# Second-table row sums over the whole TensorE array: two products a row instead of four quarters and a fold

## The reference, cut to what matters

```
def peer_ffn(h, w_q, sub_keys, u_tab, v_tab):
    blocks = h.reshape(-1, PEER_BLOCK, d)          # blocks of 128 rows
    def one_block(xb):
        q = (xb @ w_q).reshape(PEER_BLOCK, PEER_HEADS, 2, PEER_HALF)
        ...
        act = jax.nn.gelu(jnp.einsum('thkd,td->thk', u_tab[idx], xb)) * wts
        return jnp.einsum('thk,thkd->td', act, v_tab[idx])
    return lax.map(one_block, blocks).reshape(bsz, t, d)
```

## Time and profile before

| | |
|---|---|
| median of three runs | 3575.82 us |
| span of the profiled execution | 3751.8 us |
| mean granted TensorE clock in it | 0.819 |
| busy: TensorE, VectorE, ScalarE, GpSimd | 2608.3, 1998.1, 710.4, 1507.8 us |
| HBM read | 1152.84 MB, of which the software queue (gathers above all) 849.51 MB |

### The profile page before, as it was taken

How to read it: one execution, slowest core, us unless ns; L and a number is a source line. 1 busy time by engine, 2 the same in 40 slices (tenths; PEclk the granted TensorE clock), 3 DMA queues, 4 the chain that set the end, 5 groups by cost and what they waited for, 6 DMA issues and landing times.

```text
span 3751.8 us, 35602 instructions
## 1 busy us (share of the span) xinstructions
PE 2608.3 (70%) x12888; PEld 1195.8 (32%) x12888; DVE 1998.1 (53%) x5016; ACT 710.4 (19%) x1775; POOL 1507.8 (40%) x1609
## 2 busy tenths in 40 slices
PE   6687766655556675655679666556654798899998
PEld 1233222111112221111144221112311385676765
DVE  0465656656657656776422476667698436221411
ACT  1121111211112311211132112112221213020300
POOL 0025555555665666566600056666466400000000
PEclk8888888788776887676679778777877899999999
DMA  8779998999998999899923489999999776667677
GB/s 316 269 275 342 342 344 326 367 402 401 365 361 320 356 363 340 320 364 361 359 100 122 149 326 384 361 364 332 348 354 334 298 260 255 219 251 249 215 255 258
DMA packets 363676, 1156.38 MB, mean 308 GB/s; under 512 B 33712, under 2 KB 33968, under 8 KB 362476
## 3 DMA queue, kind: packets, MB, share of 16 engines
q0 software_dynamic: 232144, 849.51, 60.5%
q1 hardware_dynamic: 130940, 304.36, 22.7%
q10 hardware_dynamic: 416, 0.23, 0.0%
HBM read 1152.84 MB, written 1.15 MB: 308 GB/s over the span
## 4 chain that ended last, share of the span: by engine, by line
PE 42%; DVE 19%; DMA 14%; issue 7%; POOL 7%; another core or an unknown queue 5%; ACT 5%; SPq 0%; DVEq 0%; ACTq 0%; POOLq 0%
PE PS L1155 10%; PE PS L1089 8%; POOL BIG L2357 7%; DVE BIG L1965 7%; PE PS L1360 6%; PE PS L1378 6%; DMA BIG<-in_p_v_dram,IDX 6%; DMA BIG<-in_p_u_dram,IDX 5%; PE PS L1254 2%; PE PS L1348 1%; PE PS L1117 1%; DVE SC L2151 1%; DMA WR<-in_w_mod_dram 1%; ACT dg L1552 1%
## 5 line engine op out<-in xcount | busy, mean ns | idle before, releaser
L1155 PE MATMUL PS<-BIG,dg 64*64 64x512 f32 x6144 | 1059.3, 823 | 849.7 <-ACT dg L1552 383.5
L2357 POOL DMA_INDIRECT BIG<-in_p_u_dram,IDX x768 | 734.5, 956 | 1163.2 <-ACT PS L1539 417.8
L1965 DVE CUSTOM_DVE_ANT_0 BIG<-BIG,PS 128x1024 f32<-128x1024 f32 x768 | 927.8, 1215 | 325.8 <-DMA BIG<-in_p_u_dram,IDX 294.3
L2357 POOL DMA_INDIRECT BIG<-in_p_v_dram,IDX x768 | 732.0, 953 | 313.7 <-issue 180.6
L1155 PEld LDWEIGHTS PS<-BIG,dg 64*64 64x64 f32 x6144 | 274.9, 172 | 1520.9 <-issue 963.4
L1089 PE MATMUL PS<-WR,HT 128*128 128x512 f32 x640 | 294.4, 614 | 9.9 <-DMA WR<-in_a_w_in_dram 6.6
L1552 ACT ACTIVATE dg<-twin,ACTV 128x64 f32<-128x64 f32 x768 | 208.0, 336 | 345.2 <-PE PS L1155 149.8
L1360 PE MATMUL PS<-HT,WR 128*128 128x128 f32 x2048 | 256.1, 285 | 5.9 <-DMA WR<-in_mlp_w_dram 5.9
L1360 PEld LDWEIGHTS PS<-HT,WR 128*128 128x128 f32 x2048 | 247.3, 200 | 15.8 <-issue 8.9
L1378 PE MATMUL PS<-WR,BIG 128*128 128x512 f32 x512 | 226.0, 596 | 0.0
L1089 PEld LDWEIGHTS PS<-WR,HT 128*128 128x128 f32 x640 | 122.3, 196 | 177.0 <-issue 167.9
(11 more groups left out here) (320 smaller groups left out, 2709.7 us busy)
## 6 DMA issues: line engine op xcount, KB each, us to landing
WR<-in_mlp_w_dram SPq DMA_DIRECT2D x128, 1024.0 KB
WR<-in_w_mod_dram SPq DMA_DIRECT2D x48, 1024.0 KB
WR<-in_b_w_in_dram SPq DMA_DIRECT2D x18, 1024.0 KB
WR<-in_a_w_in_dram SPq DMA_DIRECT2D x16, 1024.0 KB
WR<-in_p_w_q_dram SPq DMA_DIRECT2D x16, 1024.0 KB
BIG<-in_dsa_w_dram POOLq DMA_DIRECT2D x16, 1024.0 KB, 7.6
BIG<-in_p_u_dram,IDX POOLq DMA_INDIRECT x768
BIG<-in_p_v_dram,IDX POOLq DMA_INDIRECT x768
```

The source lines that it names most:

```text
L1155: mm = self.e.matmul(pv[64 * i:64 * i + 64, 2 * r + n, :], dg[p, :], row[p, n * 512:n * 512 + 512], start=h == 0 and j == 0, stop=h == 7 a ...
L1965: self.e.tensor_tensor_reduce(row, row, xp, 1.0, 0.0, ALU.mult, ALU.add, m.ACTV[:, u % 4, j:j + 1]).then_inc(*self.done("dot", l, u, j))
L2357: self.e.indirect_dma_start(row, None, m.A[f"p_{table}"], bass.IndirectOffsetOnAxis(ap=m.IDX[:, u % 4, j:j + 1], axis=0)).then_inc(*m.GR.l ...
```

## The change

A v-row is summed alone, over the whole array: `dg` is the full 128x128 diagonal (from `ident`), and there are two products of 128x128 by 128x512 a row, one for each half of the width. They add into one PSUM buffer of two banks a block; there are two such buffers, so `PV` has two places. `twin` is gone, and `dg` has five buffers of 512 bytes a partition instead of six of 256. The fold is gone on ScalarE and VectorE; `gated_add` reads the sum from PSUM itself, one step later than the fold stood. The scratch of the software DMA queue shrinks to 8192 bytes a partition, where no size was given before.

```
-        self.PV = Slots([PSt[:, 4:8, :]])
+        self.PV = Slots([PSt[:, 4 + 2 * i:6 + 2 * i, :] for i in range(2)])
...
-        self.DG = Slots([sb(f"dg{i}", [128, 64]) for i in range(6)])
+        self.DG = Slots([sb(f"dg{i}", [128, 128]) for i in range(5)])
...
     def finish(self, l, b, gate, gain, shift):
         m = self.m
-        for n in range(2):
-            self.fold(l, b, n)
         self.spread(gate, "b")
...
                     self.v_gather(l, u - 1, j)
-                    if j % 2:
-                        self.v_sum(l, u - 1, j - 1, b, h)
+                    self.v_sum(l, u - 1, j, b, h)
...
-        pv = m.PV.of(l, b)
-        self.wait_ge(m.act.at("diagonal", l, u, j + 1), m.GR.landed("v", l, u, j), m.GR.landed("v", l, u, j + 1))
+        pv, row, dg = m.PV.of(l, b), m.GR.of("v", l, u, j), m.DG.of(l, u, j)
+        self.wait_ge(m.act.at("diagonal", l, u, j), m.GR.landed("v", l, u, j))
         for n in range(2):
-            for i in range(2):
-                row, dg = m.GR.of("v", l, u, j + i), m.DG.of(l, u, j + i)
-                for r in range(2):
-                    p = slice(64 * r, 64 * r + 64)
-                    mm = self.e.matmul(pv[64 * i:64 * i + 64, 2 * r + n, :], dg[p, :],
-                                       row[p, n * 512:n * 512 + 512], start=h == 0 and j == 0,
-                                       stop=h == 7 and j == 14)
+            mm = self.e.matmul(pv[:, n, :], dg[:, :], row[:, n * 512:n * 512 + 512], start=h == 0 and j == 0,
+                               stop=h == 7 and j == 15)
...
+        m.GR.free(("v", l, u, j), self.done.last())
+        m.DG.free((l, u, j), self.done.last())
...
+            self.e.tensor_tensor(t, m.PV.of(l, b)[:, n, :], m.BC.of(*gate)[:, n0:n0 + 512], ALU.mult).then_inc(
+                *self.done())
...
-    nc = _bacc.Bacc("TRN2", target_bir_lowering=False, num_devices=1)
+    nc = _bacc.Bacc("TRN2", target_bir_lowering=False, num_devices=1, dynamic_dma_scratch_size=8192)
```

More of the change, by code:

```diff
@@ L143, in __init__ @@
         self.ones = sb("ones", [128, 128])
-        self.twin = sb("twin", [128, 64])
         self.iota16 = sb("iota16", [128, 16])
@@ L327 @@
     route_pick = route_which = route_hot = route_index = route_weights = block_begin = hold = nothing
-    activate = u_gather = v_gather = u_dot = v_sum = fold = tiles = gate_rows = gate_sums = nothing
+    activate = u_gather = v_gather = u_dot = v_sum = tiles = gate_rows = gate_sums = nothing
     ctx_decay = ctx_flip = ctx_state = lat_begin = lat_decay = lat_flip = lat_scaled = lat_scores = nothing
@@ L962, in mlp_first @@
         yield
-        self.wait_ge(self.m.dve.at("folded", 1, 1, 1))
+        self.wait_ge(self.m.dve.at("added", "sum", 1, 1, 1))
         for _ in zip(range(12), mlp):
@@ L1548, in v_sum @@
         m = self.m
[L1549 to L1558, removed]
-        self.wait_ge(m.pe.at("block sum", l, b), m.dve.at("tmp free", l, b))
-        self.e.activation(m.tmp[0:64, n, :], pv[64:128, n, :], ACT.Copy).then_inc(*self.done())
-        self.e.activation(m.tmp[64:128, n, :], pv[0:64, 2 + n, :], ACT.Copy).then_inc(*self.done("fold", l, b, n))
+        dg = m.DG.take(l, u, j)
+        self.wait_ge(m.dve.at("active", l, u), *m.DG.emptied(l, u, j))
+        self.e.activation(dg[:, :], m.ident[:, :], ACT.Copy, scale=m.ACTV[:, u % 4, j:j + 1]).then_inc(
+            *self.done("diagonal", l, u, j))
     def gate_rows(self, b, j, gs):
@@ L1774, in silu @@
         m = self.m
-        self.e.tensor_tensor(m.twin[:, :], m.ident[:, 0:64], m.ident[:, 64:128], ALU.add).then_inc(*self.done("twin"))
         self.wait_ge(m.act.at("silu"))
@@ L1851, in spatial_gate @@
         m.PS.free(("spatial", use, b, hh), self.done.last())
-    def fold(self, l, b, n):
-        m = self.m
-        pv = m.PV.of(l, b)
-        if not n:
-            self.done.note("tmp free", l, b)
-        for r in range(2):
-            p = slice(64 * r, 64 * r + 64)
-            t = m.tmp[p, n, :]
-            self.wait_ge(m.act.at("fold", l, b, n), m.pe.at("block sum", l, b))
-            self.e.tensor_tensor(t, t, pv[p, 2 * r + n, :], ALU.add).then_inc(*self.done("folded", l, b, n))
-        if n:
-            m.PV.free((l, b), self.done.last())
     def gated_add(self, name, b, n0, gate, last):
@@ L1870, in gated_add @@
         if name[0] == "sum":
-            self.e.tensor_tensor(t, t, m.BC.of(*gate)[:, n0:n0 + 512], ALU.mult).then_inc(*self.done())
+            l, b, n = name[1:]
+            self.wait_ge(m.pe.at("block sum", l, b))
+            self.e.tensor_tensor(t, m.PV.of(l, b)[:, n, :], m.BC.of(*gate)[:, n0:n0 + 512], ALU.mult).then_inc(
+                *self.done())
+            if last:
+                m.PV.free((l, b), self.done.last())
         else:
```

5 lines of the change are left out of this document (1 added, 4 removed).

## The result

| | median us | lowest to highest |
|---|---|---|
| before | 3578.21 | 3573.34 to 3581.1, 4 runs |
| after | 3673.55 | 3673.43 to 3681.44, 4 runs |

The ratio is 1.0291 (95% interval 1.0270 to 1.0312): the change makes the kernel 95 us slower. The forecast was 3498 us with a range of 3350 to 3640, so the measured time lies outside that range; the rival "TensorE becomes the bound" gave 3671.

What follows compares the result with a forecast made beforehand. The prediction took the gather stream, held by v-row consumption freeing ring slots, as the bound in light stretches. Its terms -74 - 26 + 25 - 15 + 8 = -82 us, scaled by 0.953 to -78, gave 3498 us, range 3350 to 3640.

Steps and rivals of the forecast that it cites:

- TensorE becomes the bound: Rival: each row costs 0.9 us more of TensorE and in-order work behind it waits; about 3671 us, chance 0.18.
- The base (the view of the stretches): Reading of the 3751.8 us profile: four light stretches take 797 us for 548 gathers, 1.454 us a gather.
- light stretches, -74: Rounds with little but v-rows: slots come free earlier, gathers go to 1.32 us each, 723 us against 797.
- Block ends, -26: Where VectorE and ScalarE folded before the gelu: 6.5 us saved at each of four block ends.
- Price of a row: TensorE's time for one v-row's products: 1.8 to 2.5 us, against 1.38 before at the clock as granted.
- Dense stretches, +25: 217 to 423, 1272 to 1369 and the beginning of `peer(1)`: longer sums add 10, 12 and 3 us.
- Other mixed stretches, -15: Some 1150 us of other mixed rounds: gains by earlier slots, loses by longer queues; ends -110 and +130.
- Last rounds, +8: Last round of each peer, only v-rows: products +8 each, the fold falling away -4 each, together +8.
- Five diagonals instead of six, `PV` twice, the smaller scratch: Small things on ScalarE, PSUM and the DMA queue: each taken to change nothing.
- The transfers hold the pace: Rival: DMA already limits the light stretches, earlier slots only lengthen its queue; about 0, 3575 us, chance 0.13.
- The small scratch: Rival: GpSimd waits for landings, 0.15 us a gather over 1536 gathers, adding 230 us; about 3720 us, chance 0.04.
- What would show it: Signs of being right: light stretches under 1.35 us a gather, near 395 GB/s, clock above 0.8, v-sum wait under 150 us.

Runs made afterwards that it cites:

- undisturbed profile: The unchanged kernel before, profiled again on another chip: 3571.37 us, span 3570.1, where the first profiled execution spanned 3751.8 us.
- quarters with early diagonals: Kernel before with the 8192-byte scratch, ScalarE's diagonals written one pair ahead and twelve buffers instead of six: 3519.19 us, ratio 0.9858; 3674.53 us on the slow chip.
- early diagonals: ScalarE's diagonals written ahead in its order; in the changed kernel three rows ahead with eight buffers instead of five: 3573.43 us, ratio 1.0017, beside 3679.34 without.
- Six diagonals in pairs: Changed kernel with full products kept, but rows summed and freed in pairs again and six diagonals instead of five: 3740.47 us, ratio 1.0482.
- half products: Changed kernel with 256 of 512 columns per v-row product, except in a block's first and last row: 3566.35 us, ratio 0.9998.

## Why the prediction was wrong, point by point

**The base (the view of the stretches): failed, and with it the largest term.** The light stretches were read at 1.454 us a gather with a DMA share of 0.97, and the waits of the earlier trace rows as the ring's. In the undisturbed profile a light round takes 41 us, (166 + 248)/(4 + 6), 1.29 us a gather, at 409 GB/s: the 1.32 us I hoped to reach was already beaten. The term "light stretches, -74" measures -8. One of its four stretches, 1369 to 1515, was not light at all (line 1155 was 67 of TensorE's 84 busy us there): by the starts of the same gathers it went from 132 to 144 us, 12 us longer. I had the sign of it in hand: the profiled execution was 176 us above the median, and I spread that over all terms with the factor 0.953, though the light stretches alone hold 797 - 548 x 1.29 = 90 us of it. The chip on which the kernel before took 3764 us shows the same light rounds; quarters with early diagonals, four light rounds there and on the other chip:

```profile
900.00:1083.00 183.00, 96.28 (x516) 26.67 (x516) 116.36 (x280) 28.87 (x89) 119.02 (x127) 0.72 0.96 363
```

```profile
865.00:1031.00 166.00, 88.43 (x524) 25.24 (x520) 118.89 (x281) 28.86 (x89) 121.59 (x129) 0.83 1.03 408
```

**Block ends, -26: mis-sized.** The run without a fold is 4.6 us faster (between 9 us faster and 1 us slower), the one block end above 2.6 us shorter. The base was at fault here too: from the last dot product to the multiplication that same block end took 1132.98 - 1116.91 = 16.07 us in the profile I used and 8.87 in the undisturbed one. And the gate's row, which I had listed as staying, takes up most of what the fold gives back.

**Price of a row: right.** 1522.8/768 = 1.98 us, within 1.8 to 2.5, and the granted clock rose to between 0.97 and 1.00 in light stretches, above the 0.8 forecast. The undisturbed trace had 1003.9 us for line 1155, so the rows cost 519 us more of TensorE, of which 95 us (the result) to 111 (beside each other on one chip) reached the end. The sentence on the packing rule of the Trainium skill ("TensorE: Matmul & The Clock Gate", Packing small matmuls) had the direction right, with 600 us where the traces have 519.

**Dense stretches, +25: right in kind, too small.** Its three places are 222 to 422 and 1208 to 1294 of the undisturbed profile, and the beginning of `peer(1)`. They became 219, 104 and 147 us instead of 200, 86 and 142: +42, inside its ends of +8 and +60.

**Other mixed stretches, -15: the step that failed most after the base.** They hold the rest, 113 + 8 - 42 - 7 = 72 us (the block ends, the 12 us of above and the last round of `peer(1)` among them). I set their idle time on TensorE (over 400 us) against what is added, as if idle time were a store to draw on. It wasn't: much of it lay in the loop's other half, and early diagonals gave 106 us back. The earlier trace rows had the sign of it, 383.5 us of idle time before line 1155 released by ScalarE's diagonals, and I priced the diagonals only as busy time ("nothing").

**Last rounds, +8:** the last stretch of `peer(0)` went from 75 to 82 us. For one of the two rounds I had worked out +8 for the products and -4 for the fold, so +4; the fold gave little back. That of `peer(1)` was not taken by itself.

**Five diagonals instead of six, `PV` twice, the smaller scratch: nothing, right** for the scratch by its own run. By what the Trainium skill ("SBUF — State Buffer", SBUF size: 192, 224, or 256?) says of the scratch a limit on gathers in flight was possible; at 8192 bytes the run shows none. A diagonal of 128x128 took 392 ns on the mean, above the 336 to 381 I had set, and all of them 266.0 us of ScalarE instead of 208.0. Six diagonals in pairs (3740.47 us) did not help; five against six with nothing else changed, and the two places of `PV`, were not tried.

**The rivals.** "TensorE becomes the bound" had the number (3671). Its mechanism was right in one half, in-order work behind longer sums. The other half, a round's products exceeding its gathers, is at most part of it: with early diagonals the same products end within 5 us of before, though 54 us above quarters treated alike. The closeness of its number is partly luck: its +130 for mixed stretches (72 measured) was too much, its -37 and -26 for light ones and block ends too good. "The transfers hold the pace" was true of every light round. The small scratch fell. **What would show it:** light stretches under 1.35 us, near 395 GB/s (407 to 410 measured) and a clock there above 0.8 all came true and proved nothing, since the undisturbed kernel before does the first two as well; GpSimd's wait for the v-sum (247.7, not under 150) spoke.

## What to carry to other kernels

Before taking a rate from a profile whose span is 5% above the timed median, find in which stretches the excess lies; where it can't be found, those stretches' gains have a bound at zero. Idle time of an in-order engine is a reserve only if what ends it doesn't itself wait for that engine: follow each large wait one step further, to what its releaser had been waiting for. And where two engines feed each other in turns, write the small producer's work a step or two ahead in its order: with more buffers for it, that was worth 106 us in the changed kernel and 49 us in the kernel before, whose 3519.19 us are the best of these runs. And compare two forms only after giving both the same cure: with it the full products still cost 54 us.

## What the runs showed of the hardware

- The kernel before took 3568 to 3578 us on most chips and 3764 us on one; quarters with early diagonals 3519.19 and 3674.53 us, the changed kernel with them 3573.43 and 3704.49. In quarters with early diagonals four light rounds moved 408 GB/s on the one chip and 363 on the other. What differs between the chips was not found.
- More work on TensorE came with a higher clock: 127 us busy of 165 at 1.00 in the four light rounds of the changed kernel, 88 of 166 at 0.83 in the kernel before. But half products were busy 114 of 166 there at 0.65:

```profile
874.00:1040.00 166.00, 114.23 (x266) 68.07 (x265) 118.95 (x282) 36.36 (x93) 121.47 (x129) 0.65 1.03 409
```
